# A decoder layer on one core: the experts' inputs sorted from a normed copy of h, in the holes of the blocks

## The reference, cut to what matters

```python
h = x + jnp.concatenate([oa, ob], axis=-1) @ w_out[l]
return h + _moe(_rmsnorm(h, norm2_w), w_router, b_router, w_gate_up, b_gate_up, w_down, b_down)

# _moe: hn = _rmsnorm(h, norm2_w)
logits = hf @ w_router + b_router            # 256 tokens x 32 experts
top_v, top_e = lax.top_k(logits, TOP_K)      # 4 experts for a token
gates = jax.nn.softmax(top_v, axis=-1)
# the rows of each expert are brought together in blocks, and for each block
gu = xblk @ w_gu[e] + b_gu[e]                # 1024 -> 2048
gate = jnp.minimum(gu[:, :D_FF], 7.0); up = jnp.clip(gu[:, D_FF:], -7.0, 7.0)
act = (up + 1.0) * gate * jax.nn.sigmoid(1.702 * gate)
y = act @ w_dn[e] + b_dn[e]                  # 1024 -> 1024, times the row's gate, added to its token
```

## Time and profile before

| | |
|---|---|
| device time, median of three | 1200.06 us |
| device time of the profiled execution | 1196.28 us |
| its span, first to last instruction | 1194.5 us |
| mean granted TensorE clock | 0.973 |
| TensorE busy (matmul) | 1102.0 us, 92% |
| VectorE busy | 280.7 us, 23% |
| ScalarE busy | 168.1 us, 14% |
| read from HBM | 424.29 MB, 357 GB/s over the span |
| chain that ended last | PE 61%, DMA 31%, DVE 5% |

### The profile page before, as it was taken

How to read it: one execution, slowest core, us unless ns; L and a number is a source line. 1 busy time by engine, 2 the same in 40 slices (tenths; PEclk the granted TensorE clock), 3 DMA queues, 4 the chain that set the end, 5 groups by cost and what they waited for, 6 DMA issues and landing times.

```text
span 1194.5 us, 12955 instructions
## 1 busy us (share of the span) xinstructions
PE 1102.0 (92%) x5122; PEld 480.2 (40%) x5122; DVE 280.7 (23%) x651; ACT 168.1 (14%) x283; POOL 8.5 (1%) x29
## 2 busy tenths in 40 slices
PE   8999989999999999998799999989899999889997
PEld 7856655654434343344233333322233323222332
DVE  3642344232312121214211111111112111111111
ACT  3422333200100000101000100000001100100101
POOL 1000000000000000000000000000000000000000
PEclk9999989799999999999799999999999999999999
DMA  9592132889799999997499999999999999999996
GB/s 323 106 393 82 71 141 88 353 331 372 313 364 430 403 429 380 422 370 334 189 418 427 438 425 436 428 432 431 425 431 431 435 430 433 427 434 422 428 425 264
DMA packets 37330, 427.34 MB, mean 358 GB/s; under 512 B 6163, under 2 KB 8308, under 8 KB 17460
## 3 DMA queue, kind: packets, MB, share of 16 engines
q1 hardware_dynamic: 34724, 426.33, 86.2%
q10 hardware_dynamic: 2576, 0.59, 0.2%
HBM read 424.29 MB, written 2.62 MB: 357 GB/s over the span
## 4 chain that ended last, share of the span: by engine, by line
PE 61%; DMA 31%; DVE 5%; issue 2%; SPq 1%; ACT 0%; DVEq 0%; ACTq 0%
DMA store<-in_w_gate_up_dram 22%; PE bank L1797 21%; PE bank L1842 13%; DMA store<-in_w_down_dram 9%; PE bank L1387 5%; PE bank L1719 4%; PE bank L1583 4%; PE bank L1394 4%; PE bank L1458 2%; PE bank L1785 2%; PE bank L1735 1%; DVE flow L1253 1%; DVE flow L1259 1%; DMA store<-in_w_in_dram 1%; DVE flow L1226 1%
## 5 line engine op out<-in xcount | busy, mean ns | idle before, releaser
L1797 PE MATMUL bank<-store,flow 128*64 128x512 f32 x2048 | 452.5, 599 | 4.5 <-DMA store<-in_w_gate_up_dram 4.5
L1797 PEld LDWEIGHTS bank<-store,flow 128*64 128x64 f32 x2048 | 144.8, 138 | 310.7 <-issue 300.4
L1842 PE MATMUL bank<-store,flow 128*64 128x512 f32 x1008 | 237.1, 621 | 33.3 <-DVE flow L1259 23.7
L1242 DVE TENSOR_SCALAR flow<-bank 128x512 f32<-128x512 f32 x32 | 22.1, 692 | 645.1 <-PE bank L1797 645.1
L1842 PEld LDWEIGHTS bank<-store,flow 128*64 128x64 f32 x1008 | 72.6, 142 | 173.8 <-issue 147.4
L797 ACT ACTIVATE flow<-flow 128x512 f32<-128x512 f32 x32 | 20.1, 630 | 526.4 <-DVE flow L1242 526.4
L1735 PE MATMUL bank<-qkT 64*128 64x512 f32 x248 | 61.6, 615 | 0.0
L813 ACT COPY qkT<-bank 128x512 f32<-128x512 f32 x32 | 18.7, 585 | 275.2 <-PE bank L1842 275.1
L1387 PE MATMUL bank<-store 128*128 128x512 f32 x128 | 56.4, 592 | 0.0
L1394 PE MATMUL bank<-store 128*128 128x256 f32 x192 | 42.7, 380 | 2.0 <-DMA store<-in_w_in_dram 2.0
L1813 PE MATMUL bank<-ident,flow 128*128 128x128 f32 x128 | 20.6, 284 | 24.6 <-DVE flow L1253 24.6
(11 more groups left out here) (326 smaller groups left out, 651.4 us busy)
## 6 DMA issues: line engine op xcount, KB each, us to landing
store<-in_w_gate_up_dram SPq DMA_DIRECT2D x38, 4096.0 KB, 25.4
store<-in_w_down_dram SPq DMA_DIRECT2D x62, 2048.0 KB, 16.3
store<-in_w_gate_up_dram SPq DMA_DIRECT2D x52, 2048.0 KB, 12.7
store<-in_w_in_dram SPq DMA_DIRECT2D x7, 2048.0 KB, 22.3
store<-in_w_out_dram SPq DMA_DIRECT2D x1, 4096.0 KB, 18.7
flow<-in_w_down_dram SPq DMA_DIRECT2D x1, 2048.0 KB, 19.2
store<-in_w_down_dram SPq DMA_DIRECT2D x2, 1024.0 KB, 34.0
bias_by_distance<-flow SPq DMA_DIRECT2D x1, 1536.0 KB
```

The costliest lines, as they stand in the source:

```text
L1797: ins = mm(dst[SLOTS * hf:SLOTS * (hf + 1), :], xgT[:, c:c + SLOTS], store[:, slot_at(k, odd) + c0:slot_at(k, odd) + c0 + 512], start=Fals ...
L1842: ins = mm(dst[SLOTS * hf:SLOTS * (hf + 1), :], turned[:, c:c + SLOTS], w[:, hf * 512:(hf + 1) * 512], start=f == 0, stop=f == KT - 1)
```

## The change

It changes where h and its copy lie, what the chunk products read, and when they run.

- **Places.** `hx` moves to the start of `flow`, where chunks 0 and 1 will be written. The place it had, behind `extra`, is now `arena`. After the attention part it holds `hn`, and later chunks 6 and 7.
- **`h_normed(t)`**, new on ScalarE: one copy per tile from `hx` to `hn`, scaled by the reciprocal norm and put in the experts' column order. `h_rows` now returns 128 neighbouring columns of `hn`. `SEL` and `chosen` are plain 0/1, so the last multiplication of `choose` goes.
- **Sums begun with h.** `add_residual` adds h to the four banks before anything else does: (0, 0) and (0, 1) where `keep_clock` stood, (1, 0) and (1, 1) after `gate_up(0)`. `combine` no longer starts a sum, `add_mixture` adds the bias alone. The ranks move from bank 1 to bank 7.
- **Chunks.** The second half goes right behind `turn_act`, into bank 5, and VectorE's two `sorted_rows` both stand behind its copy of `actT`. Chunk 6 goes with block 9 and is held in `up` and `sg`; chunk 7 goes between block 9's two `down`s. `chunk_end` is gone. TensorE waits at the block's end for VectorE to have read the chunk.
- **Tables.** `late_tables` and its parts on VectorE and ScalarE move from between blocks 9 and 10 to between 19 and 20. The order of SyncE's queue is not touched.

```diff
         flow = sb("flow", [P, T * D + 2 * SLOT + T * D + 12 * S])
-        arena1 = flow[:, 0:T * D].rearrange("p (t d) -> p t d", t=T)
+        hx = flow[:, 0:T * D].rearrange("p (t d) -> p t d", t=T)
         extra = flow[:, T * D:T * D + 2 * SLOT]
-        hx = flow[:, T * D + 2 * SLOT:2 * T * D + 2 * SLOT].rearrange("p (t d) -> p t d", t=T)
+        arena = flow[:, T * D + 2 * SLOT:2 * T * D + 2 * SLOT]
+        arena1 = arena.rearrange("p (t d) -> p t d", t=T)
...
         def h_rows(t, k):
-
-            half, i = divmod(k, 4)
-            return hx[:, t, 512 * half:512 * (half + 1)].rearrange("q (p i) -> q i p", i=4)[:, i]
+            return hn[:, t, k * P:(k + 1) * P]
...
+            def h_normed(t):
+
+                act.wait_ge(h_rstd, t + 1)
+                hnr.mark(act.activation(hn[:, t, :].rearrange("q (h i p) -> q h i p", h=2, i=4),
+                                        hx[:, t, :].rearrange("q (h p i) -> q h i p", h=2, i=4), ACT.Copy,
+                                        scale=nrm[:, 1, 2 + t:3 + t]))
...
+            def sorted_rows(chunk):
+
+                for half in range(2):
+
+                    dve.wait_ge(ch_psum, 16 if chunk == 7 else 2 * chunk + half + 1)
+                    src, w2 = heads(bank[6 - half][:]), wide(w2p[:, 4 * half:4 * half + 4], P)
+                    if chunk == 6:
+
+                        hd.mark(dve.tensor_tensor(heads(hold[half]), src, w2, ALU.mult))
+                    else:
+                        xs.mark(dve.tensor_tensor(sorted_half(chunk, half), src, w2, ALU.mult))
...
-                if chunk is not None:
-                    dve.wait_ge(ch_psum, 2 * chunk + 1)
-                    sorted_rows(P * chunk, P, 0, 4, bank[6])
                 dve.wait_ge(actT_psum, b + 1)
                 dve.tensor_copy(actT_last if last else actT, bank[4][:]).then_inc(actT_ready, 1)
                 if chunk is not None:
-                    dve.wait_ge(ch_psum, 2 * chunk + 2)
-                    sorted_rows(P * chunk, P, 4, 4, bank[6])
+                    sorted_rows(chunk)
...
+            choose(7)
+            sorted_rows(7)
+            dve.wait_ge(held, 2)
+            for half in range(2):
+                xs.mark(dve.tensor_copy(sorted_half(6, half), heads(hold[half])))
+            dve.wait_ge(xs_ready, 16)
+            with dve.Fori(FINE_BLOCKS, TABLE_BLOCK) as b:
+                expert_block(b)
...
+            def add_residual(t, hf):
+
+                mm(bank[2 * t + hf][:], ident[:], hx[:, t, 512 * hf:512 * (hf + 1)], start=True, stop=False,
+                   skip_group_check=True)
...
-                pe.wait_ge(chosen_ready, 8 * T)
-                pe.wait_ge(y_ready, FINE_BLOCKS)
-                chunk_end(range(4))
...
-                chunk_end(range(4, KT))
-                pe.wait_ge(xs_ready, 16)
...
                 turn_act(b)
+                if chunk is not None:
+                    chunk_half(chunk, 1)
                 pe.wait_ge(actT_ready, b + 1)
...
                 down(b, 0)
+                if isinstance(chunk, int) and chunk == 6:
+                    chunk_half(7, 0)
+                    chunk_half(7, 1)
+                    chunk = 7
+                down(b, 1)
                 if chunk is not None:
-                    chunk_half(chunk, 1)
-                down(b, 1)
+
+                    pe.wait_ge(xs_ready, 14 if isinstance(chunk, int) and chunk == 7 else 2 * chunk + 2)
...
+            expert_block(FINE_BLOCKS - 2, 0, 5)
+            expert_block(FINE_BLOCKS - 1, 1, 6)
+            with pe.Fori(FINE_BLOCKS // 2, TABLE_BLOCK // 2) as pair:
+                later_block(2 * pair, 0)
+                later_block(2 * pair + 1, 1)
             late_tables()
```

More of the change, by code:

```diff
@@ L25 @@
 LATE_BLOCKS, LAST_ORDER = 20, 24
+TABLE_BLOCK = 20
 SLOTS = 64
@@ L243, in hybrid_layer @@
         chosen = [qk[:, 1, S:S + P], rows_sel[:]]
-        chosen_end = [sg[:, S * t:S * (t + 1)] for t in range(T)]
         oh_cur = qk[:, 1, S + T * SLOTS:S + T * SLOTS + SLOTS]
@@ L1222, in _ @@
[L1222 to L1228 removed]
+                    for t in range(T):
+                        ins = dve.scalar_tensor_tensor(out=chosen[t], in0=iota_p[:],
+                                                       scalar=pos4[:, 4 * t + k:4 * t + k + 1], in1=chosen[t],
+                                                       op0=ALU.is_equal, op1=ALU.add)
+                        if k == TOP_K - 1:
+                            cr.mark(ins)
+                        elif t:
+                            st.step(ins)
+                        else:
+                            st.mark(ins)
@@ L1230, in expert_block @@
             def expert_block(b, last=False, chunk=None):
                 if chunk is not None:
-                    choose(chunk, chosen)
+                    choose(chunk)
                 for t in range(T):
@@ L1278, in _ @@
                 (st.step if j < S // SLOTS - 1 else nb.mark)(ins)
-            for c in range(2):
-                choose(6 + c, [chosen_end[t][:, P * c:P * (c + 1)] for t in range(T)])
             dve.wait_ge(end_psum, 1)
@@ L1714, in chunk_half, with combine @@
                     pe.wait_ge(chosen_ready, T * c + T)
-                if not (isinstance(c, int) and (c, half) == (0, 0)):
-                    pe.wait_ge(xs_ready, 2 * c + half)
+                if isinstance(c, int) and c == 7:
+                    pe.wait_ge(held, half + 1)
+                elif not isinstance(c, int) or c:
+                    pe.wait_ge(xs_ready, 2 * c + (half - 1))
                 for i in range(4):
                     for t in range(T):
-                        ins = mm(bank[6][:, i * P:(i + 1) * P], h_rows(t, 4 * half + i), chosen[t], start=t == 0,
-                                 stop=t == T - 1)
+                        ins = mm(bank[6 - half][:, i * P:(i + 1) * P], h_rows(t, 4 * half + i), chosen[t],
+                                 start=t == 0, stop=t == T - 1)
                 ins.then_inc(ch_psum, 1)
-            def chunk_end(ks):
-                for k in ks:
-                    dst = bank[(6, 7, 4, 5)[k // 2]][:, (k % 2) * S:(k % 2 + 1) * S]
-                    for t in range(T):
-                        ins = mm(dst, h_rows(t, k), chosen_end[t], start=t == 0, stop=t == T - 1)
-                ins.then_inc(ch_psum, 1)
-            def combine(first=False, final=False):
+            def combine(final=False):
                 turned = SGT_last if final else SGT
@@ L1827, in down @@
                 at = last_at if last else slot_at(8)
-                early = isinstance(b, int)
+                early = isinstance(b, int) and b < 2
                 if early and (b, half) == (1, 0):
@@ L1857, in expert_block @@
                 pe.wait_ge(y_ready, b)
-                combine(first=isinstance(b, int))
+                combine()
                 rest(b, chunk)
```

100 lines of the change are left out of this document (47 added, 53 removed).

## The result

The kernel after takes 1150.62 us (median of four runs, 1150.48 to 1152.74), the kernel before 1198.99 on the same chip (four runs, 1196.88 to 1200.4; the fourth moved the median from 1200.06). The ratio is 0.9602, 95% interval 0.9582 to 0.9622. The forecast was 1152 us in a range of 1143 to 1170. Of the profiled executions, before took 1196.28 us and after 1150.48. The span of the profiled execution fell from 1194.5 to 1148.7 us.

The account below looks back on a forecast made before the run. The prediction took the weights' stream at 430 GB/s as the bound: idle time falling from 57.6 to 9 us (2 + 4.2 + 1 + 2) gains 48.4 us, 1148 us profiled, 1152 at the median, range 1143 to 1170.

Parts of the forecast that it names:

- The bound: Whole kernel: the weights' stream at 430 GB/s bounds it; the end moves by the idle time saved, 57.6 us between 239 and 598.
- The halves: Chunk products: contiguous h makes a half take 1.8 us instead of 3.74; rival, they stay at 3.74: 1177 us, chance 0.10.
- The holes: Chunk halves placed in TensorE's waits at block ends: a chunk costs 1.7 us instead of 7.2; ten blocks take 282 us.
- The hand-over: Gathers before block 0: contiguous reads take 2.2 us each instead of 3.7 and 3.8, giving 3 us, bounds 0 and 5.
- The start of the stream: First blocks: stream idles 2 us since 239, then 4.2 us waiting for down places and block ends.
- The tables: Pause before block 20: 9.3 us plus 3 for a slow start; stream idles 1 us, plus 2 for the queue's order changes.
- The sum: Whole stream: idles 9 us where it idled 57.6, a gain of 48.4 us; 1148 us profiled, 1152 at the median.
- TensorE's waits: Sign of being right: TensorE waits for the down weights from about block 5.
- a slice under 400 GB/s between 10 and 38: Sign of being wrong: the DMA rate falls below 400 GB/s in one of those profile slices.
- The pause paid: Rival at the tables: they take 24 us, or places are taken because TensorE had been ahead; 1163 us, chance 0.12.
- The slower stream: Rival for the early blocks: 2 MB pieces miss 430 GB/s; 4% less over nine rounds gives 1162 us, chance 0.08.
- The clock: Rival in blocks 3 to 19: granted clock falls to 0.50 after weight waits; 1229 us with four such blocks, chance 0.04.

Follow-up runs that it names:

- e7_morework: Kernel after with four unread products of 256 columns at the end of each of blocks 10 to 19, 1.9 us a block: 1161.42 us, ratio 0.9696 to before.
- e1_strided: Kernel after with h copied in its own column order, so chunk products and gathers read it with a step of 16 bytes: 1181.5 us, ratio 0.9879 to before.
- e2_between: Kernel after with the second half of chunks 0 to 6 put back between the two down products: 1157.64 us, ratio 0.9687 to before.
- e9_order25: Kernel after, tables still at block 20, with the queue's changes of order at blocks 25 and 26 instead of 20 and 24: 1146.33 us, ratio 0.9572 to before.
- e10_tables16: Kernel after with the tables between blocks 15 and 16, a repeat of an earlier run: 1143.13 us, ratio 0.9552 to before.

## Why the prediction was right, and where it was not

- **The bound.** Right. Idle time of the stream from 239 to 1100 went from 58.1 to 14.0 us, and the span with it; the table of twelve kernels shows the same sum for each. e7_morework is the test from the other side: of 19 us of added work on TensorE 9.5 are paid, as idle time of the stream.
- **The halves.** Right: 1.78 us for the 1.8 taken, 192 ns a load. e1_strided shows that the way h is read is the cause. A rule by the number of columns alone would have left 3.74 us. The reading behind it, that the clock does not set a load's time, holds only for the strided load; see the next but one.
- **The holes.** Right: a chunk costs 13.32 - 11.72 = 1.60 us for 1.7 forecast. In block 9 the wait of 0.4 us for chunk 7 did not come; the `down`s start 7.36 us apart (501.51 and 508.87), which leaves 3.7 for chunk 7. Block 10 starts at 512.45, forecast 518; most of the difference is the next point. The ten blocks take 282.3 us (230.18 to 512.45), forecast 282.
- **The hand-over.** Mis-sized: "That gives 3 us; bounds 0 (...) and 5 (the clock rises as well)". The first piece is issued 7.6 us sooner, above both. On the two timelines the first gather starts 0.5 us sooner, the second follows it after 2.95 us in place of 6.01, block 0's bias follows that after 2.08 in place of 4.12 (228.10 to 230.18, and 231.64 to 235.76), and the first piece is released 4.75 us after the bias in place of 6.76. The granted clock is 1.00 throughout, where it was 0.50 from 227 to 240. The prediction had treated the clock as given; e1_strided shows that it came with the strided loads. Its 2.2 us for a contiguous gather at half clock rests on no row, and the rows speak against it: where the clock is 0.50 in e2_between (521 to 523), a contiguous load takes 333 ns, as much as a strided one, and a pair of products comes every 0.43 us. By that, an estimate from products with 128 moving columns where the gather has 64, its eight pairs would take 3.4 us, and with the clock left at 0.50 the copy would have gained little here.
- **The start of the stream.** Forecast 2 + 4.2 us of idle time behind 239, measured 5.0. The 2 are not there, since the stream ran again before 239; the 4.2 became 1.8 up to 280 and 3.0 from 280 to 320.
- **The tables.** The pause was 9.25 us for 9.3, and block 20 took 4.1 us more than the next (30.86 us from bias to bias against 26.7), where 3 were forecast for a slow clock. Of these, 2.5 stand directly behind the pause, and 1.6 in `down`, 8.72 us for 7.09, which blocks 23 and 26 show as well, without a pause. Its price was mis-sized: "1 us with the issue" for the pause and "2 us, between 0 and 5" for the changes of order, 3 in all; measured 9.6. The two had been priced apart, each against a TensorE in step with the stream; but the first change of order falls on the block behind the pause, and the second comes four blocks later, before TensorE has caught up. e9_order25 and e10_tables16 show both parts near nothing where they are apart.
- **The sum.** Behind 239 the stream idled 14.6 us for 9.2 forecast, and ahead of 239 it gained 2.4 us that the forecast did not have. That is 3.0 us short of the forecast: the tables cost 6.6 more, the first blocks 0.8 more, the start 4.4 less. It fits the profiled executions, 1150.48 us for 1148. Between the medians the miss shrinks to 1.4 us the other way, 1150.62 for 1152, because 3.8 us were added for how far before's profiled execution lay under its median, while after's lay at its own. So much of the closeness is luck.
- **TensorE's waits.** Forecast from about block 5, they begin at block 12 (585.77). TensorE's pace is not the reason, as the 282.3 us show. In ten blocks it gains only 11 us on the stream's 293, and how far ahead the stream was at the start the prediction had not counted. The sign "a slice under 400 GB/s between 10 and 38" did appear, twice behind the tables (365 and 376) and once at slice 10 (389); the place of the error was named by it, though not its cause.
- **The rivals.** The halves: e1_strided shows what strided loads give in this order, 1181.5. The pause paid: not here, but e7_morework is that case, and the condition is the reverse of the one given: the pause is paid when TensorE had not been ahead. The slower stream: 426 to 435 GB/s in slices 11 to 27. The clock: 0.98 from 239 to 1100, with twelve waits for down weights, the longest 1.9 us.

## What to carry to other kernels

When a stream of loads bounds the kernel, count where it idles, and price every edit by that; what an engine saves or wastes counts only where a place comes free late. Price disturbances together if they can fall within a few rounds of each other: what each asks of the slack is added, and the slack comes back slowly (2 us a block here). A copy that makes a stationary operand contiguous can pay twice, in the loads themselves and in the granted clock; the first only where the clock is high.

## What the runs showed of the hardware

- A float32 weight load of h, 128 columns, with a step of 16 bytes takes 329 to 330 ns, with 64 or 128 moving columns, at a granted clock of 0.50 (the gathers of before) and of 1.00 (the chunk products of before and e1_strided). Where it reads neighbouring numbers it takes 192 ns at a granted clock of 1.00 (after), but 333 at 0.50 (e2_between, 520.6 to 523.1). So the step costs only where the clock is high. ScalarE pays for the step once: 2.13 us for the 1024 numbers of a tile, beside the router's steps.
- The granted clock at the hand-over follows the same edit: 1.00 (2.4 GHz) from 229 to 232 us with contiguous loads, 0.50 (1.2 GHz) with strided ones, in before and in e1_strided, though PE shows as busy for the whole window in all three. It falls inside the first strided gather, which starts at 225.6: before 227 in before (0.65 from 226 to 227), before 228 in e1_strided (0.89 from 227 to 228). It is 1.00 again from 240 and from 242. Which feature of the strided loads does it was not tested.
- The clock is also low behind the pause: 0.50 from 808 to 812, and 15.50 us for `gate_up(20)`, where 13.95 is usual. It falls in e2_between behind the wait of 3.33 us: from 520.36 to 523.35 a pair of chunk products comes every 0.43 us instead of every 0.22. And it falls where TensorE waited only for VectorE, 1.0 and 0.8 us: 0.52 from 912 to 914, `down` 8.75 us for 7.09. In all, from 598 to 1114, with twelve waits for down weights of up to 1.9 us, it is 0.96.
- One core draws 430 GB/s for hundreds of microseconds with TensorE 90% busy (before, 598 to 1114). The Trainium skill, "Perfetto Trace Analysis", section "Roofline", names about 435 GB/s as what one core's DMA engines can move; the trace agrees with 430.
